# A transformer kernel: MLP weights in pieces of two couples, the forget gate as one product, buffers laid out anew

## What is computed

```python
# odd mixer (16 heads of 64), h = rmsnorm(x)
q, k, v, f = split(h @ odd_w_in)              # f: 16 gate columns, the last of 3088
lf = log_sigmoid(f + odd_b_forget)            # one log gate per token and head
cum = cumsum(lf, axis=tokens)
logits = q @ k.T * 64 ** -0.5 + cum[i] - cum[j]   # causal
x = x + softmax(logits) @ v @ odd_w_out
# MLP of either layer
x = x + square(relu(rmsnorm(x) @ mlp_w1)) @ mlp_w2    # 1024 -> 4096 -> 1024
```

## Time and profile before

| | |
|---|---|
| median of 3 runs | 1897.1 us |
| the profiled execution | 1897.14 us |
| its span | 1895.3 us |
| mean granted TensorE clock | 0.987 |
| PE busy | 1824.0 us (96%) |
| DVE, ACT busy | 504.7 us, 346.3 us |
| DMA | 558.43 MB, mean 295 GB/s |

### The profile page before, as it was taken

How to read it: one execution, slowest core, us unless ns; L and a number is a source line. 1 busy time by engine, 2 the same in 40 slices (tenths; PEclk the granted TensorE clock), 3 DMA queues, 4 the chain that set the end, 5 groups by cost and what they waited for, 6 DMA issues and landing times. The chain is left out here.

```text
span 1895.3 us, 21658 instructions
## 1 busy us (share of the span) xinstructions
PE 1824.0 (96%) x8601; PEld 995.0 (52%) x8602; DVE 504.7 (27%) x1093; ACT 346.3 (18%) x684; POOL 5.3 (0%) x10
## 2 busy tenths in 40 slices
PE   6999799999999999999999998999999999999998
PEld 4857433333333333333333335768885466688843
DVE  1654411111111011011011104543015543210355
ACT  3221311111111111111111113233000032220000
POOL 0000000000000000000000000000000000000000
PEclk9999799999999999999999999999999999999999
DMA  9986589999999999999999999324345443133253
GB/s 400 313 172 269 219 351 431 431 432 432 432 432 432 432 431 432 431 427 431 432 431 432 431 429 321 109 108 143 133 147 186 155 177 134 45 133 136 88 175 111
DMA packets 101170, 558.43 MB, mean 295 GB/s; under 512 B 16920, under 2 KB 33789, under 8 KB 74365
## 3 DMA queue, kind: packets, MB, share of 16 engines
q1 hardware_dynamic: 98660, 553.19, 71.8%
q10 hardware_dynamic: 2458, 4.50, 1.8%
HBM read 552.43 MB, written 5.23 MB: 294 GB/s over the span
## 5 line engine op out<-in xcount | busy, mean ns | idle before, releaser
L1340 PE MATMUL ps<-ring,xs 128*64 128x512 f32 x2112 | 466.9, 593 | 8.3 <-DMA ring<-in_w_up 5.2
L1340 PEld LDWEIGHTS ps<-ring,xs 128*64 128x64 f32 x2112 | 150.7, 137 | 312.7 <-issue 293.1
L1393 PE MATMUL ps<-ring,actT 128*64 128x512 f32 x1056 | 233.9, 595 | 0.0
L2112 PE MATMUL ps<-hT,ring 128*128 128x256 f32 x1024 | 222.0, 379 | 0.2 <-ACT hT L1590 0.2
L2112 PEld LDWEIGHTS ps<-hT,ring 128*128 128x128 f32 x1024 | 194.3, 190 | 27.0 <-ACT hT L1590 0.6
L2137 PE MATMUL ps<-ring 128*128 128x512 f32 x448 | 192.8, 592 | 0.0
L1393 PEld LDWEIGHTS ps<-ring,actT 128*64 128x64 f32 x1056 | 72.9, 137 | 158.7 <-issue 131.9
L1465 DVE TENSOR_SCALAR hT<-ps 128x512 f32<-128x512 f32 x33 | 22.8, 692 | 446.9 <-PE ps L1340 446.9
L2137 PEld LDWEIGHTS ps<-ring 128*128 128x128 f32 x448 | 85.0, 190 | 105.8 <-issue 105.7
L1905 PE MATMUL ps<-hT,ring 128*128 128x256 f32 x512 | 122.2, 394 | 6.8 <-ACT hT L1590 5.5
L1905 PEld LDWEIGHTS ps<-hT,ring 128*128 128x128 f32 x512 | 98.2, 196 | 26.1 <-issue 10.3
(11 more groups left out here) (426 smaller groups left out, 1528.7 us busy)
## 6 DMA issues: line engine op xcount, KB each, us to landing
ring<-in_w_up SPq DMA_DIRECT2D x64, 2048.0 KB, 23.4
ring<-in_w_down SPq DMA_DIRECT2D x64, 2048.0 KB, 24.5
ring<-in_w_gate SPq DMA_DIRECT2D x64, 2048.0 KB, 23.0
ring<-in_mlp_w SPq DMA_DIRECT2D x16, 2048.0 KB, 7.6
ring<-in_mlp_w SPq DMA_DIRECT2D x32, 1024.0 KB, 5.2
ring<-in_w_mod SPq DMA_DIRECT2D x8, 2048.0 KB, 15.9
ring<-in_odd_w_in SPq DMA_DIRECT2D x6, 2048.0 KB, 7.6
ring<-in_w_mod SPq DMA_DIRECT2D x8, 1024.0 KB, 14.5
```

The lines of the kernel that those rows point to most:

```text
L1340: mm = pe.matmul(ps[SLOTS * half:SLOTS * (half + 1), bank, :], xs[:, c % 4, c // 4 * SLOTS:(c // 4 + 1) * SLOTS], weights(v, 8 * part + c) ...
L1393: mm = pe.matmul(ps[SLOTS * half:SLOTS * (half + 1), Y, :], actT[:, f % 4, f // 4 * SLOTS:(f // 4 + 1) * SLOTS], weights(v, 16 + f)[:, hal ...
L2112: mm = pe.matmul(ps[:, bank + f // 2, (f % 2) * SEQ:(f % 2 + 1) * SEQ], mlp_w1[layer][g % 2][:, c, f * P:(f + 1) * P], hT[:, c, :], start= ...
```

## The change

**The second MLP weight** is fetched in pieces of two couples. A piece has two DMAs of 1 MB, one for each half of the hidden channels, and 8 KB per partition each. There are two piece slots with one semaphore each. Piece p is asked for when `couple_ps` reaches 2p - 2, and DVE and PE wait for both DMAs of a piece.

**The forget gate** is one product: 16 matmuls with 128 tokens of `hT` as the stationary operand and the 16 gate columns as the moving one, straight into tokens by gates. The copy, the adding matmuls, their semaphores and the constant go.

**The order** of the odd mixer's start is another on PE and DVE. **The buffers** are laid out in another order and without padding. In the built program `ring` started at byte 17,152 of each partition and now starts at 32,448.

```diff
-for _name, _n in (("ident", P), ..., ("etri", EXPERTS), ("gate16", 16), ("pad", 6),
+for _name, _n in (("ident", P), ..., ("etri", EXPERTS),
...
-    wf = pairs[:, 4, :].rearrange("p (c h) -> p c h", c=C)
-    bf = pairs[:, 5, 64:80]
-    gate_part = std[:]
+    wf = pairs[:, 4, 0:C * 16].rearrange("p (c h) -> p c h", c=C)
+    bf = pairs[:, 4, 128:144]
...
-    mlp_w2 = [[slots(a, 2) for a in at] for at in ((8, 10, 4, 6), (0, 2, 12, 14))]
+    mlp_w2 = [[slots(a, 4).rearrange("p (h j) n -> p h j n", h=2) for a in at] for at in ((8, 4), (0, 12))]
...
-            def couple(layer, c):
-                sp.dma_start(mlp_w2[layer][c % 4], W2[layer][:, :, c, :]).then_inc(w2_in[c % 4], 16)
+            def piece(layer, p):
+                for h in range(2):
+                    sp.dma_start(mlp_w2[layer][p % 2][:, h], W2[layer][:, h, 2 * p:2 * p + 2, :]).then_inc(w2_in[p % 2], 16)
...
-            sp.dma_start(wf, odd[:, :, 3 * D - 16:]).then_inc(fox_in, 16)
+            sp.dma_start(wf, odd[:, :, 3 * D:]).then_inc(fox_in, 16)
...
-            for c in range(4, PAIRS):
-                sp.wait_ge(couple_ps, c - 3)
-                couple(0, c)
+            for p in range(2, PAIRS // 2):
+                sp.wait_ge(couple_ps, 2 * p - 2)
+                piece(0, p)
...
-                pe.wait_ge(w2_in[c % 4], 64 * layer + 16 * (c // 4 + 1))
+                pe.wait_ge(w2_in[c // 2 % 2], 128 * layer + 32 * (c // 4 + 1))
                 pe.wait_ge(split_ok, 8 * (PAIRS * layer + c + 1))
...
-            for c in range(C):
-                q = 32 * (c % 4)
-                mm = pe.matmul(ps[q:q + 32, 1, 0:SEQ], wf[:, c, :], hT[:, c, :], start=(c < 4), stop=(c >= 4))
-            mm.then_inc(fp_ps, 1)
+            for i in range(QT):
+                for c in range(C):
+                    mm = pe.matmul(ps[:, 0, i * 16:(i + 1) * 16], hT[:, c, i * P:(i + 1) * P], wf[:, c, :], start=(c == 0), stop=(c == C - 1))
+            mm.then_inc(fz_ps, 1)
             pe.wait_ge(fqk_in[1][0], 16)
             fox("fk0", w_fk[0], 0)
-            pe.wait_ge(fp_ok, 1)
-            for i in range(QT):
-                mm = pe.matmul(ps[:, 0, i * 16:(i + 1) * 16], gate_part[:, i * P:(i + 1) * P], cst(m, "gate16"), start=True, stop=True)
-            mm.then_inc(fz_ps, 1)
             fox("fq1", w_fq[0], 128)
-            fox("fk1", w_fk[0], 128)
             pe.wait_ge(lf_ok, 2)
...
             mm.then_inc(cum_ps, 1)
+            fox("fk1", w_fk[0], 128)
+            scores_f(0)
             fox("fq2", w_fq[0], 256)
-            scores_f(0)
             fox("fk2", w_fk[0], 256)
...
-            v.tensor_copy(gate_part, ps[:, 1, 0:SEQ]).then_inc(fp_ok, 1)
...
             v.wait_ge(cum_ok, 2)
+            fox_biased(0)
             fox_query(2)
-            fox_biased(0)
             attn.norm(v, 12)
...
+    m.consts = m.sb("consts_sb", [P, LASTING])
+    m.early = m.sb("early_consts", [P, NCONST - LASTING])
+    m.ring = m.sb("ring", [P, 4 * PARTS, D])
...
-    pad = m.sb("pad", [P, PAD])
-    m.ring = m.sb("ring", [P, 4 * PARTS, D])
```

More of the change, by code:

```diff
@@ L35 @@
 PARTS = 9
-PAD = 16
 HD = 64
@@ L60 @@
 _at = 0
-for _name, _n in (("ident", P), ("ones", P), ("tri", QT * SEQ), ("iota", P), ("causal", QT * SEQ), ("cmpvalid", QT), ("etri", EXPERTS), ("gate16", 16), ("pad", 6),
+for _name, _n in (("ident", P), ("ones", P), ("tri", QT * SEQ), ("iota", P), ("causal", QT * SEQ), ("cmpvalid", QT), ("etri", EXPERTS),
                   ("twin", HD), ("heads16", 8), ("swap", P), ("ccos", P), ("csin", P), ("stri", QT * SEQ),
-                  ("cos", SEQ), ("sin", SEQ), ("ncos", QT * SEQ), ("nsin", QT * SEQ), ("quad", EXPERTS), ("pad_last", 32)):
+                  ("cos", SEQ), ("sin", SEQ), ("ncos", QT * SEQ), ("nsin", QT * SEQ), ("quad", EXPERTS)):
     CONST[_name] = (_at, _n)
@@ L1739, in stage_second @@
     fval_in, fqk_in = [m.sem(f"s_fval_in{j}") for j in range(2)], [[m.sem(f"s_{n}{j}_in") for j in range(2)] for n in ("fq", "fk")]
-    w1_in, w2_in = [m.sem(f"s_w1{b}_in") for b in range(2)], [m.sem(f"s_w2{b}_in") for b in range(4)]
+    w1_in, w2_in = ([m.sem(f"s_{n}{b}_in") for b in range(2)] for n in ("w1", "w2"))
     zeroed = m.sem("zeroed")
@@ L1748, in stage_second @@
         m.sem(f"c_{n}") for n in ("ps", "bias", "peak", "sub", "exp", "sum", "inv", "gated", "ready", "pt", "taken"))
-    st_ps, st_std, st_ok, fp_ps, fp_ok, fz_ps, z_ok, e_ok, lf_ok, cum_ps, cum_ok = (
-        m.sem(f"od_{n}") for n in ("st_ps", "st_std", "st_ok", "fp_ps", "fp_ok", "fz_ps", "z_ok", "e_ok", "lf_ok", "cum_ps", "cum_ok"))
+    st_ps, st_std, st_ok, fz_ps, z_ok, e_ok, lf_ok, cum_ps, cum_ok = (
+        m.sem(f"od_{n}") for n in ("st_ps", "st_std", "st_ok", "fz_ps", "z_ok", "e_ok", "lf_ok", "cum_ps", "cum_ok"))
     sems = [m.sem(f"turn_{n}") for n in ("pair_ps", "x_ok", "h_ok", "sq_ok", "acc_ok", "scaled")]
@@ L1770, in quarters @@
     def quarters(layer, c):
-        w = mlp_w2[layer][c % 4]
-        return w[:, 0, LO], w[:, 0, HI], w[:, 1, LO], w[:, 1, HI]
+        w = mlp_w2[layer][c // 2 % 2]
+        return w[:, 0, c % 2, LO], w[:, 0, c % 2, HI], w[:, 1, c % 2, LO], w[:, 1, c % 2, HI]
     def hidden(c):
@@ L1822, in group @@
                 sp.dma_start(mlp_w1[layer][g % 2], W1[layer][:, :, 512 * g:512 * g + 512]).then_inc(w1_in[g % 2], 16)
-            def couple(layer, c):
-                sp.dma_start(mlp_w2[layer][c % 4], W2[layer][:, :, c, :]).then_inc(w2_in[c % 4], 16)
+            def piece(layer, p):
+                for h in range(2):
+                    sp.dma_start(mlp_w2[layer][p % 2][:, h], W2[layer][:, h, 2 * p:2 * p + 2, :]).then_inc(w2_in[p % 2], 16)
             group(0, 0)
             sp.wait_ge(proj_ps, 1 + ORDER.index("mq3"))
-            couple(0, 0)
-            couple(0, 1)
+            piece(0, 0)
             sp.wait_ge(proj_ps, 1 + ORDER.index("mk3"))
@@ L1833, in _ @@
             sp.wait_ge(attn.biased, 12)
-            couple(0, 2)
-            couple(0, 3)
+            piece(0, 1)
             odd = stack(t["odd_w_in_2"][0])
             sp.wait_ge(pair_ps, 4)
-            sp.dma_start(wf, odd[:, :, 3 * D - 16:]).then_inc(fox_in, 16)
+            sp.dma_start(wf, odd[:, :, 3 * D:]).then_inc(fox_in, 16)
             sp.dma_start(bf, bcast_row(t["odd_b_forget_2"], 16)).then_inc(fox_in, 16)
@@ L1866, in _ @@
             sp.wait_ge(pair_ps, 12)
-            for c in range(4):
-                couple(1, c)
+            piece(1, 0)
+            piece(1, 1)
             for g in range(2, GROUPS):
@@ L1871, in _ @@
                 group(1, g)
-            for c in range(4, PAIRS):
-                sp.wait_ge(couple_ps, PAIRS - 2 + c - 3)
-                couple(1, c)
+            for p in range(2, PAIRS // 2):
+                sp.wait_ge(couple_ps, PAIRS - 2 + 2 * p - 2)
+                piece(1, p)
             out = stack(t["out"][0])
@@ L2633, in split @@
                 base = 8 * (PAIRS * layer + c)
-                v.wait_ge(w2_in[c % 4], 64 * layer + 16 * (c // 4 + 1))
+                v.wait_ge(w2_in[c // 2 % 2], 128 * layer + 32 * (c // 4 + 1))
                 v.wait_ge(sqr_ok, GROUPS * layer + 5 + c // 4)
@@ L2811, in program @@
     m.one = m.sb("one", [P, 1])
+    m.ps = m.stack.enter_context(nc.psum_tensor("ps", [P, 8, 512], F32))
+    m.init = m.lasting("init")
     m.silu = m.sb("silu", [P, C, 2])
-    m.g2c = m.sb("g2c", [P, C])
-    pad = m.sb("pad", [P, PAD])
-    m.ring = m.sb("ring", [P, 4 * PARTS, D])
-    m.x = m.sb("x_sb", [P, QT, D])
-    m.hT = m.sb("hT", [P, C, SEQ])
     m.spare = m.sb("spare", [P, D])
     m.xT = m.sb("xT", [P, C, SEQ])
[L2820 to L2823, removed]
+    m.g2c = m.sb("g2c", [P, C])
     for stage in STAGES:
```

12 lines of the change are left out of this document (5 added, 7 removed).

## The result

The changed kernel takes 1912.6 us (median of 4 runs, 1911.5 to 1914.9) against 1896.8 before: ratio 1.0081 (95% interval in brackets here and below: [1.0069, 1.0093]), 15.8 us slower between the medians. The forecast was 1903.4 with a range to 1909.0. The direction was right, the size was not: 6.3 us were forecast. The profiled execution took 1914.77 us, its span is 1913.0 (before 1895.3), so there are 17.7 us to find in the traces.

What follows compares the result with a forecast made beforehand. DMA was taken to bound the expert stage with PE right behind, and PE everything from 1151 us on. Pieces +4.8, gate +2.1 and order -0.6 gave +6.3 us on 1897.1, so 1903.4 us, range 1898.2 to 1909.

Steps and rivals of the forecast that it cites:

- The addresses: Expert stage, where DMA sets the pace: the ring's new start, 192 bytes past a multiple of 256, costs nothing.
- The rival: Expert stage: the ring's new start makes each 16 KB packet 7.1 ns longer, 10.9 us more, 1914.3 us in all; 7%.
- The rival's own lever: Expert stage: 1,536 packets an engine, so each ns more per packet costs 1.54 us in full.
- The reading that I put against it: Earlier trace: 512-byte packets into `wv`, at starts of every multiple of 32, took 27 ns, as aligned ones did.
- The pieces: End of each MLP layer's down products: PE stops 2.4 us for the last piece, +4.8 us (0 to 6.0).
- The breaks at middle pieces: Down products: middle pieces hide with 1.0 us to spare; PE breaks there would show the prediction wrong.
- a rival with 10%: Behind the two MLP stops PE's clock falls: 2 x 1.7 us more, 1906.8 us; 10%.
- one stop in the earlier trace that kept the clock: From 1174 to 1180 us PE was idle for 2.5 us and kept the full clock.
- the forecast's own spread: Whole kernel: 1901.5 to 1905.5 us, from a landing of 7.4 to 8.2 and a gate of 1.5 to 2.5.
- The gate: Forget gate on PE: 32 added instructions take 3.5 us, removed ones 1.36, net +2.1 us (1.5 to 2.5).
- The order: First scores: the first turn of probabilities starts 0.30 us sooner and is 0.30 shorter, -0.6 us (0 to -0.6).
- cover for the log gates: Odd mixer's start: log gates are there by 1546.5, PE asks at 1549.1, so the cover stays 2.6 us.

Runs made afterwards that it cites:

- +128 bytes: Kernel before with 48 in place of 16 floats of padding, so the ring begins 128 bytes past a multiple of 256: ratio 1.0023, +5.0 us.
- the spread gate: Kernel before with the one-product gate, its 16 matmuls spread between the first key's projection matmuls, order of scores as before: ratio 1.0016, +3.4 us.

## Why the prediction was wrong, by its own steps

**The addresses: "so I cost the addresses at nothing".** This step failed, and its 0 is the first missing term. Ten traces with the ring on the boundary reach the first down product at 1426.8 to 1431.8 us (mean 1429.4), five with it off at 1433.3 to 1435.5 (mean 1434.7): 5.3 us. The rival's own lever, 1.54 us for each ns, gives 5.7 for 3.7 ns. How near the two are is in part luck. Of the 5.3 us, 4.0 lie within the expert stage (-0.1 behind it), and 1.4 ahead of its first matmul, where the ten traces differ by 2.8 us among themselves. Between medians the edit costs 3.1 (layout alone) to 5.0 us (+128 bytes). The rival had the right place and the right lever. Its price of 7.1 ns was nearly twice what was measured, because it priced 192 bytes more by the rate of all others, and 32 bytes cost as much as 192.

The reading that I put against it, 27 ns for 512-byte packets at every start, was made rightly: by their own records all 814 packets took 27 ns. It did not hold for other packets. Right behind them, in the same trace, 914 packets of 512 bytes at 1159 to 1161 us, by the order of issue those of the second transfer into the same rows, took 27 to 44 ns, 29.5 in the mean. In the changed kernel the 1,000 packets of 512 bytes at 1145 to 1149.5 us, from the transfer into the ring that was on the boundary before, took 27 to 41, mean 32.0. Why the first transfer was spared is open. The reading also compared small packets and asked nothing of those of 16 KB that set the pace. I gave the case 7%; a price of 0 from a single transfer, on a term with a lever of 1.54 us per ns, did not deserve it.

**The pieces: +4.8, one stop of 2.4 us a layer.** Mechanism, place and releaser were right, and the stops measured 2.0 to 2.5 in eight of ten cases (3.4 and 3.8 where an instruction fetch fell into the pair's landing, which the sum had no term for). The breaks at middle pieces, named as what would prove the step wrong, came only with late pairs and were 0.2 to 0.6 us. What was missed is the clock: behind seven of the ten stops it is at 0.50 for 3.4 us, 1.7 us each. That was a rival with 10%, and its size was right. It was held down by one stop in the earlier trace rows that kept the clock, and the other stop there had lost it. (The lower end of the forecast's own spread, 1901.5, does not come out of its terms: a landing of 7.4 and a gate of 1.5 give 1902.4. Nothing hangs on it.)

**The gate: +2.1.** The instructions cost +2.1, shown by the spread gate. The clock that falls in the unbroken run costs another 3.3, in no rival. The sum put the 32 instructions at the pace of the 12 in the earlier trace rows, at a clock that it took as given because PE is busy.

**The order: -0.6.** The turn became as short and as early as forecast, in the kernel after and alone. The whole -0.6 shows with the new gate in both kernels (269.1 to 268.5 us); alone, the order's cover for the log gates is gone, and it wins nothing.

Together: 6.3 forecast + 3.7 for the addresses + 3.3 for the clock at the gate + 1.7 for the clock behind layer 1's stop + 1.4 for its late pair (3.8 against 2.4) - 0.3 for layer 0's shorter stop = 16.1 of the 17.7 us. Another 0.5 are breaks at two middle pieces. The last 1.1 us are not assigned: 0.6 in layer 0's down products and 0.5 in layer 1's, in both near the stop.

## What to carry over

Where a transfer sets the pace of a long stage, a layout change is an edit of that stage: keep the buffer's start on the boundary it had, or measure one packet size at the new start before costing it at nothing. Where one wait covers two transfers, the consumer pays for the later one plus both pieces of its own work; a semaphore for each took the stop away at the same request times. Where a landing has a microsecond of cover, look in the trace for instruction packets in it: they made it up to 1.6 us later. And a stop or a run of very short matmuls on TensorE is priced with the stretch of half clock that may follow, so such matmuls belong between long ones.

## What the runs showed of the hardware

- Packets of 16 KB into SBUF took 611 ns in the mean with the buffer's start on a multiple of 256 bytes and 615 to 616 with it 32, 128 or 192 past one.
- Two DMAs of 1 MB issued 0.4 us apart were both there after 7.2 to 7.9 us, and after 8.1 to 9.1 when an instruction packet (8 KB, 0.3 us, or 16 KB, 0.9 to 1.1 us) fell behind their first microsecond: 18 pairs of 18.
- The granted clock fell to 0.50 (1.2 GHz) for 3.4 to 6.8 us while PE was busy without a pause, when 32 instructions with 16 moving columns stood in a row: five traces of five. With the same 32 between matmuls of 256 columns it stayed at 1.00. The Trainium skill (TensorE: Matmul & The Clock Gate, The HAM clock gate) tells of the fall for an idle engine; here the engine shows as busy.
- Behind a single stop of 2.0 to 3.8 us it fell in seven cases of ten. What tells the three others apart is open: all three were layer 0's, in kernels with the whole change.
